# Mixture-of-experts stage: experts in order of their token counts, three short ones with tokens listed twice, blocks of up to 1024 columns, four split slots

## The chip, the cores and the metric

The kernel runs on one core of a Trainium2 chip. The metric is the device time of one execution in microseconds, as the median of several runs; less is better. The core has TensorE (matmuls into PSUM banks of 512 float32 columns), VectorE, ScalarE, GpSimd and the sync engine SyncE, whose queue starts most of the loads.

## The reference

Two transformer blocks of two layers each over 256 tokens of width 1024. All stages but the last are the same in both kernels. The last stage is a mixture of experts: eight experts, each token goes to its best two.

```python
def swiglu(h, w_gate, w_up, w_down):
    a = jnp.einsum('bsd,df->bsf', h, w_gate)
    u = jnp.einsum('bsd,df->bsf', h, w_up)
    return jnp.einsum('bsf,fd->bsd', jax.nn.silu(a) * u, w_down)

def moe_swiglu(h, w_router, w_gate, w_up, w_down):
    ...
    for e in range(N_EXPERTS):
        out = out + combine[..., e:e + 1].astype(h.dtype) * swiglu(h, w_gate[e], w_up[e], w_down[e])
```

Gate and up are 1024 x 2816, down is 2816 x 1024, all float32: 34.6 MB an expert. `combine` is zero but for the two experts of a token.

## The kernel before

**Products in three matmuls.** Float32 operands are split into a high part (rounded to the format that the matmul takes) and a low part (what is left): ScalarE writes `w_hi` (L1892), VectorE `w_lo` (L977). `product` (L2351 to L2353) then issues high by high, high by low and low by high. The tokens' rows are split in the same way (`hT_hi`, `hT_lo`), and so are the hidden values (`hid_hi`, `hid_lo`).

**Weights in tiles.** SyncE loads weight tiles of 128 x 2048 into six raw slots of `slab`, each when VectorE's low part of the tile that was there is done. A tile is then split into one of three split slots of `w_hi` and `w_lo`, each when TensorE has used the tile that was there (`w_used`). There are 33 tiles an expert.

**An expert.** Its tokens are at most 128: VectorE makes a 0/1 matrix from their places (`lists`), TensorE makes the list of token numbers from it (`list_places`), GpSimd fetches the rows by an indirect transfer (`fetch`), TensorE turns them (`turn_fetched`, L2841). The 2816 hidden columns go in six steps of at most 512: `rows_up(j)` makes the step's up rows in one bank and its gate rows in another, ScalarE takes the silu (L2279), VectorE multiplies (L1757), `turn(j)` transposes the product in pieces of 128 columns (L2470), ScalarE and VectorE split it (L2179, L1559), and `sums` adds its share of the down product in banks 2 and 3. Between a step's rows and its turn stand the sums of the step before. ScalarE scales the finished sums into `y_out` (L2263), and GpSimd adds them to `y_rows` in HBM by an indirect transfer that adds (`scatter`, L924). The last expert's sums go back by matmuls instead. Experts run in the order of their numbers; `each_expert` writes out the first and the last and loops over pairs between them. The order of the work on every engine is written out by hand. If an expert has more than 128 tokens, `flag` makes the whole stage run a second time.

Of the kernel before, what the change touches and what calls it, by code (L numbers as in the profile page):

```python
# [9 lines left out]
F32 = mybir.dt.float32  # L10
# [7 lines left out]
P = 128  # L18
D = 1024
# [47 lines left out]
F_WIDE = 512  # L67
# [22 lines left out]
X_MACT, X_MACT2, X_G, X_YE = 4096, 4864, 4608, 5376  # L90
# [114 lines left out]
def build(nc, A, out):  # L205
    ctx = ExitStack()
    with ctx:
# [10 lines left out]
        hT_lo = sb("hT_lo", [P, KC, SEQ], F32R)  # L218
        big = sb("big", [P, ADA])
# [13 lines left out]
        posi = sb("posi", [P, TT], I32)  # L233
# [7 lines left out]
        flag = sb("flag", [1, 1], I32)  # L241
# [77 lines left out]
        last_g, rows_out, rows_in = sem("last_g"), sem("rows_out"), sem("rows_in")  # L319
# [29 lines left out]
        MT = 3 * MJ  # L349
        MS = 1 + (FF2 - F_GATED) // F_WIDE  # L350
# [4 lines left out]
        def ff_tiles(l):  # L355
            return 4 * steps(l) if l < DEPTH else MT
# [165 lines left out]
        def expert_ring(ring, i, p, t0, loads0, ahead=2):  # L522


            done = MT * p + ahead
            ring.t, ring.i, ring.raw, ring.split = t0 + i * (2 * MT) + done, done, MORE_RAW, 3
            ring.at = 0 if isinstance(i, int) and i == 0 and p == 0 and t0 == ring.start else -MORE_RAW
            ring.loads = [c + i * (2 * MT // MORE_RAW) + sum(k % MORE_RAW == s for k in range(done))
                          for s, c in enumerate(loads0)]
# [10 lines left out]
        def expert_steps(eng, ring, step, before_last):  # L540

            with eng.Fori(0, MS - 3) as jj:
                ring.enter(jj, 6)
                step(jj + 2)
            ring.leave(MS - 3)
            before_last()
            step(MS - 1)

        def narrow(j):

            return isinstance(j, int) and j == 0

        def wide_at(j):

            return j * F_WIDE - F_GATED

        def expert_after(t0, loads0):

            return t0 + NE * MT, [c + NE * MT // MORE_RAW for c in loads0]
# [19 lines left out]
        def listed(p, b):  # L579

            return slice(KC // 2 * p + 2 * b, KC // 2 * p + 2 * b + 2)
# [5 lines left out]
        def by_two(src):  # L587

            return src.rearrange("p (a n) -> p a n", a=2)
# [4 lines left out]
        def _(sp):  # L594
# [82 lines left out]
            for l in LAYERS:  # L677
# [57 lines left out]
                else:  # L735
                    stage(MORE_RAW)

                    def expert_loads(t0, loads0, n0):
# [5 lines left out]
                        def body(i, p, n, first, last):  # L744
# [3 lines left out]
                            def step(j, norm=False):  # L748
                                cols(wu, wide_at(j + 1), F_WIDE)
                                if norm:  # L750

                                    sp.wait_ge(sc_done, 2 * (UNIT0[l] + UNITS[l]))
# [2212 lines left out]
```

## Time and profile before

| | |
|---|---|
| median of 3 runs | 1911.68 us (1910.37 to 1918.38) |
| profiled execution, span | 1912.1 us |
| TensorE matmul, busy | 1824.1 us, 95% |
| VectorE | 1416.6 us, 74% |
| ScalarE | 1122.6 us, 59% |
| GpSimd | 392.8 us, 21% |
| HBM read | 497.49 MB |
| the chain that ended last, by engine | PE 83%, DVE 7%, issue 6%, ACT 3%, POOL 1% |

The span runs from the first to the last instruction of one profiled execution; no other time of that execution is given. Shares of busy time are means over stages with different limits, so the stage that the change touches has to be read by itself: the experts, from about 1134 us to the end.

### The profile page before, as it was taken

Reading aid. Unit: us, or ns where it says so; the run is one execution under the profiler, and the core shown is the slowest. Engines: PE = TensorE matmul, PEld = TensorE weight load, DVE = VectorE, ACT = ScalarE, POOL = GpSimd, SP = SyncE. Lnnn points to the kernel's source line nnn. Section 1 sums busy time; section 2 is a strip of 40 time slices with the busy share of each in tenths; the row PEclk is TensorE's granted clock in tenths of the full one; section 3 lists DMA queues with packets and bytes.
Section 4 is the critical chain, followed back from the end, with each engine's and each line's share of the span. In section 5 each row is a group of like instructions: output and inputs, shape, how many; then the busy total and the mean of one; then the engine's idle time right before and its main releaser. Section 6 shows DMA issues by size and latency. Waiting matters only on the chain.

```text
span 1912.1 us, 26024 instructions
## 1 busy us (share of the span) xinstructions
PE 1824.1 (95%) x8799; PEld 1486.2 (78%) x8799; DVE 1416.6 (74%) x1631; ACT 1122.6 (59%) x1296; POOL 392.8 (21%) x315
## 2 busy tenths in 40 slices
PE   7899999989999998899989879999999999999997
PEld 6678886868888786688878667888888888888885
DVE  5748874466976586644458758889888888888897
ACT  6745444564443464443345537777777777777775
POOL 3722203463212363200046500000000000000000
PEclk9999999999999999999999989999999999999999
DMA  8348884418987341455544258999999999999994
GB/s 271 111 161 327 343 342 147 149 54 323 344 347 275 91 152 45 154 195 179 192 154 142 69 187 334 386 376 386 380 384 376 383 383 381 380 374 381 381 387 167
DMA packets 237934, 506.45 MB, mean 265 GB/s; under 512 B 23304, under 2 KB 74720, under 8 KB 231712
## 3 DMA queue, kind: packets, MB, share of 16 engines
q1 hardware_dynamic: 225664, 492.91, 70.9%
q0 software_dynamic: 3008, 10.32, 2.0%
q10 hardware_dynamic: 9184, 2.23, 0.5%
q8 instruction: 43, 0.70, 0.1%
q14 instruction: 35, 0.29, 0.0%
HBM read 497.49 MB, written 7.91 MB: 264 GB/s over the span
## 4 chain that ended last, share of the span: by engine, by line
PE 83%; DVE 7%; issue 6%; ACT 3%; POOL 1%; DMA 0%; POOLq 0%; SPq 0%; DVEq 0%; ACTq 0%
PE bank L2351 25%; PE bank L2353 25%; PE bank L2352 25%; PE bank L2470 2%; ACT slab L2042 1%; PE bank L2789 1%; DVE slab L1290 1%; PE bank L2561 1%; PE bank L2539 1%; ACT w_hi L1892 1%; PE bank L2521 1%; POOL w_lo L826 1%; DVE x L1074 0%; PE bank L2572 0%; DVE slab L1271 0%
## 5 line engine op out<-in xcount | busy, mean ns | idle before, releaser
L977 DVE TENSOR_TENSOR w_lo<-slab,w_hi 128x2048 fp32r<-128x2048 f32 x369 | 847.8, 2308 | 214.3 <-ACT w_hi L1892 213.3
L1892 ACT ACTIVATE w_hi<-slab 128x2048 fp32r<-128x2048 f32 (+2 forms) x421 | 796.6, 1898 | 329.0 <-PE bank L2353 256.3
L2351 PE MATMUL bank<-w_hi,hT_hi 128*128 128x512 f32 (+3 forms) x1664 | 649.4, 390 | 14.2 <-DVE hT_lo L1012 4.4
L2352 PE MATMUL bank<-w_lo,hT_hi 128*128 128x512 f32 (+3 forms) x1664 | 638.0, 383 | 0.0
L2353 PE MATMUL bank<-w_hi,hT_lo 128*128 128x512 f32 (+3 forms) x1664 | 637.9, 383 | 0.0
L2351 PEld LDWEIGHTS bank<-w_hi,hT_hi 128*128 128x128 f32 x1664 | 316.0, 190 | 77.9 <-DVE w_lo L977 8.8
L2353 PEld LDWEIGHTS bank<-w_hi,hT_lo 128*128 128x128 f32 x1664 | 315.5, 190 | 59.7
L2352 PEld LDWEIGHTS bank<-w_lo,hT_hi 128*128 128x128 f32 x1664 | 316.3, 190 | 55.3
L826 POOL TENSOR_TENSOR w_lo<-slab,w_hi 128x512 fp32r<-128x512 f32 (+2 forms) x208 | 262.4, 1295 | 381.3 <-ACT w_hi L1892 361.6
L2351 PE MATMUL bank<-w_hi,hid_hi 128*128 128x512 f32 x680 | 265.6, 391 | 0.7 <-DVE w_lo L977 0.7
L2353 PE MATMUL bank<-w_hi,hid_lo 128*128 128x512 f32 x680 | 265.0, 390 | 0.0
L2352 PE MATMUL bank<-w_lo,hid_hi 128*128 128x512 f32 x680 | 264.5, 389 | 0.0
L2351 PEld LDWEIGHTS bank<-w_hi,hid_hi 128*128 128x128 f32 x680 | 127.6, 188 | 29.2 <-issue 2.3
L2353 PEld LDWEIGHTS bank<-w_hi,hid_lo 128*128 128x128 f32 x680 | 127.6, 188 | 26.7
L2352 PEld LDWEIGHTS bank<-w_lo,hid_hi 128*128 128x128 f32 x680 | 127.7, 188 | 26.3
L924 POOL DMA_INDIRECT y_rows<-slab,posi x7 | 16.6, 2367 | 515.6 <-ACT slab L2263 515.6
L901 POOL TENSOR_TENSOR slab<-slab 128x512 f32<-128x512 f32 x32 | 60.0, 1893 | 251.6 <-ACT slab L2188 251.6
L1577 DVE SCALAR_TENSOR_TENSOR big<-slab,csilu,big 128x2048 f32<-128x2048 f32 x42 | 103.5, 2473 | 0.0
L2042 ACT ACTIVATE slab<-slab,att 128x256 f32<-128x256 f32 x144 | 71.4, 499 | 52.3 <-DVE att L1271 43.0
L2179 ACT ACTIVATE hid_hi<-bank 128x512 fp32r<-128x512 f32 (+1 forms) x95 | 47.6, 527 | 46.1 <-PE bank L2470 46.1
L1290 DVE TENSOR_TENSOR slab<-slab,att 128x512 f32<-128x512 f32 x56 | 52.7, 942 | 5.8
L1271 DVE CUSTOM_DVE_ANT_0 slab<-bank,const 128x256 f32<-128x256 f32 x88 | 31.9, 417 | 33.4 <-PE bank L2521 33.3
(252 smaller groups left out, 1232.0 us busy)
## 6 DMA issues: line engine op xcount, KB each, us to landing
slab<-in_w_exp_gate SPq DMA_DIRECT2D x176, 512.0 KB, 7.0
slab<-in_w_exp_up SPq DMA_DIRECT2D x176, 512.0 KB, 7.5
slab<-in_w_exp_down SPq DMA_DIRECT2D x176, 512.0 KB, 7.1
slab<-in_w_ada SPq DMA_DIRECT2D x48, 1024.0 KB, 5.5
slab<-in_w_mlp_in SPq DMA_DIRECT2D x64, 512.0 KB, 5.4
slab<-in_w_mlp_out SPq DMA_DIRECT2D x64, 512.0 KB, 9.0
slab<-in_w_in SPq DMA_DIRECT2D x56, 512.0 KB, 5.0
slab<-in_w_out SPq DMA_DIRECT2D x32, 512.0 KB, 4.6
```

What stands on the lines that cost most here:

```text
L826: ins = pool.tensor_tensor(w_lo[:, q, o], raw(s)[:, o], w_hi[:, q, o].bitcast(F32), ALU.subtract)
L901: pool.tensor_tensor(scr(X_ACT2 + t * F_UP, F_UP), a, a, ALU.mult).then_inc(sq_done, 1)
L977: dve.tensor_tensor(w_lo[:, q, 0:n], raw(s)[:, 0:n], w_hi[:, q, 0:n].bitcast(F32), ALU.subtract).then_inc(lo_dve, 1)
L1290: dve.tensor_tensor(p, p, r[:, s, :].unsqueeze(2).broadcast_to([P, TT, SEQ]), ALU.mult).then_inc(nrm_done, 2)
L1577: ins = dve.scalar_tensor_tensor(acc, w, c, acc, ALU.mult, ALU.add)
L1892: act.activation(w_hi[:, q, 0:n], raw(s)[:, 0:n], ACT.Copy).then_inc(hi_done, 1)
L2042: act.activation(p, p, ACT.Exp, bias=att[:, 1, j, t:t + 1], scale=-1.0, accum_out=att[:, 2, j, t:t + 1]).then_inc(ex_done, 1)
L2179: act.activation(to_hi[:, f0:f0 + n, t * P:(t + 1) * P], src, ACT.Copy).then_inc(hidh_done, 1)
L2351: pe.matmul(dst, a_hi, b_hi, start=start, stop=False)
L2352: pe.matmul(dst, a_hi, b_lo, start=False, stop=False)
L2353: return pe.matmul(dst, a_lo, b_hi, start=False, stop=stop_)
L2470: ins = pe.transpose(dst[t][:, f * P:(f + 1) * P], scr(src + t * width_ + f * P, P), ident)
```

## The change

- The experts are sorted by their numbers of tokens in a new piece of code on VectorE (`sort`). Expert 0 is always first. Of the others the four with the most tokens take the odd places 1, 3, 5 and 7, and the three with the fewest the places 2, 4 and 6. These three are the short ones. SyncE reads the order from `order` and picks the weights by it.
- A short expert has at most 64 tokens, and its list names each of them twice, in columns 0 to 63 and 64 to 127. Its gate is made in full, with three matmuls a product, for both copies. Its up product takes as rows 64 high parts and 64 low parts of the same tokens, so two matmuls (by `w_hi` and by `w_lo`) do for three. Both halves are multiplied by the gate, and the turn adds them: instead of a transpose, each chunk of 128 columns takes two matmuls by halves of the identity matrix. The hidden values are then stacked in the same way for the down product, and the two halves of its result are added to `y_rows` by two indirect transfers. The down product of the last block, which is issued in the next expert's body, stays at three matmuls, with `hid_lo` cleared.
- All experts work in three blocks of 768, 1024 and 1024 hidden columns, in two banks for gate (0, 1) and two for up (4, 5), up first. A row of a load of gate or up is 4 KB (3 KB in the first block), where it was 2 KB (1 KB in the first step). There are 36 tiles an expert, 12 of them narrower than 2048 columns or half full.
- Four split slots instead of three.
- SyncE's loads are written out expert by expert instead of looped over.

```diff
+E_WIDTH = (768, 1024, 1024)
+MS = len(E_WIDTH)
+MT = 36
+SHORT = P // 2
+SHORT_AT = (2, 4, 6)
...
-                    ring.stage(3 if l < MOE else MORE_RAW, 3, 1)
+                    ring.stage(*((3, 3, 1) if l < MOE else (MORE_RAW, SPLIT, 0)))
...
+            def down_chunks(j):
+
+                return ((0, 2), (2, 2), (4, 1), (5, 1)) if j == 0 else ((0, 2), (2, 2), (4, 2), (6, 2))
...
+                                for k in range(2):
+                                    sp.dma_start(d[:, k:k + 1, :], w[:, 2 * b + k:2 * b + k + 1, E_FROM[j]:E_FROM[j] + E_WIDTH[j]]
+                                                 ).then_inc(loaded, 16)
...
+                for a, o in enumerate((slice(0, SHORT), slice(SHORT, P)) if at in SHORT_AT else (slice(0, P),)):
+                    pool.wait_ge(scattered, done - (16 if at not in SHORT_AT else 32) + 16 * a)
...
+                        hidden_low(0)
+                        if short:
+                            dve.wait_ge(w_used, FREE_SPLIT + EXPERT0 + n * MT + 8)
+                            dve.tensor_scalar(hid_lo[:, :, :], ones[:, 0:1].unsqueeze(2).broadcast_to([P, 4, SEQ]), 0.0, None, ALU.mult
+                                              ).then_inc(hid_zero, 1)
+                        if first:
+                            dve.nop().then_inc(hid_zero, 1)
+                        if first and n0 == 0:
+                            sort()
...
+                        def both(dst, hi_, lo_, q, s, start, stop_):
+
+                            if lo_ is None:
+                                pe.matmul(dst, hi_, w_hi[:, q, s], start=start, stop=False)
+                                return pe.matmul(dst, hi_, w_lo[:, q, s], start=False, stop=stop_)
+                            return product(dst, hi_, lo_, w_hi[:, q, s], w_lo[:, q, s], start, stop_)
...
+                                    if halved:
+                                        l_hi, l_lo = rows_k[:, SHORT:SHORT + P], None
+                                    else:
+                                        l_hi, l_lo = rows_k[:, 0:P], rows_k[:, P:2 * P]
...
+                                if short:
+                                    to = banks[f // 4][:, f % 4 * P:f % 4 * P + SHORT]
+                                    pe.matmul(to, src, ident[:, 0:SHORT], start=True, stop=False)
+                                    ins = pe.matmul(to, src, ident[:, SHORT:P], start=False, stop=True)
+                                else:
+                                    ins = pe.transpose(banks[f // 4][:, f % 4 * P:(f % 4 + 1) * P], src, ident)
...
+                        inner(0)
+                        gate(0)
+                        if first:
+                            inner(1)
+                            pe.wait_ge(ix_made, 2 * n + 2)
+                            turn(0)
+                        else:
+                            if p == 1:
+                                pe.wait_ge(hid_zero, i + (1 + (len(SHORT_AT) + 1) * turn_))
+                            sums(-1, False)
+                            turn(0)
+                            inner(1)
+                        gate(1)
```

Where instructions move, the order on the engine shows it. First TensorE, before, from the end of one step's sums over its turn into the next step's up rows (every expert, inside the loop; L2470 is the turn, L2351 to L2353 a product):

```order
L2351 MATMUL bank<-w_hi,hid_hi 128x512
L2352 MATMUL bank<-w_lo,hid_hi 128x512
L2353 MATMUL bank<-w_hi,hid_lo 128x512
L2468 REGISTER_ALU
L2470 MATMUL bank<-const,slab 128x128 x4
L2884 REGISTER_ALU
L2404 ISA
L2351 MATMUL bank<-w_hi,hT_hi 128x512
```

And the same place in a short expert of the change, with the numbers of the banks (L3113 and L3114 are the two halves of the turn, L3054 and L3055 the two matmuls of an up product; the sums ahead of this turn are those of the expert before, in three matmuls, L2533 to L2535):

```order
L2535 MATMUL bank3<-w_hi,hid_lo 128x512
L3109 ISA
L3113 MATMUL bank0<-const,big 128x64
L3114 MATMUL bank0<-const,big 128x64
...
L3048 REGISTER_ALU
L3054 MATMUL bank4<-w_hi,hT_hi 128x512
L3055 MATMUL bank4<-w_lo,hT_hi 128x512
L3054 MATMUL bank5<-w_hi,hT_hi 128x512
L3055 MATMUL bank5<-w_lo,hT_hi 128x512
```

The turn of four transposes has become one of six (in the other blocks eight) pairs of narrow matmuls, and the products after it have lost their third matmul.

Second VectorE, before, in the first expert (L977 is a low part of a weight tile, L1757 the multiplication, L1559 the low part of the hidden values, L1706 and L1700 the list of the next expert):

```order
L1741 TENSOR_TENSOR hT_lo<-bank,hT_hi 128x512 x2
L1730 TENSOR_SCALAR listed_cols<-bank,listed_cols 128x1
L1731 COPY listed_cols<-bank 128x1
L1733 SCALAR_TENSOR_TENSOR posi<-bank,listed_cols 128x1
L977 TENSOR_TENSOR w_lo<-slab,w_hi 128x2048
L1757 TENSOR_TENSOR slab<-slab,bank 128x256
L977 TENSOR_TENSOR w_lo<-slab,w_hi 128x2048 x2
L1559 TENSOR_TENSOR hid_lo<-bank,hid_hi 128x2x128
L977 TENSOR_TENSOR w_lo<-slab,w_hi 128x2048 x2
L1706 COPY listed_cols<-big 128x2
L1700 TENSOR_SCALAR slab<-const,big 128x128 x2
L977 TENSOR_TENSOR w_lo<-slab,w_hi 128x2048
```

And in the change (L1847 is the low part of a tile, L1857 the multiplication, L1874 the hidden low part; L1771 to L1795 are the sort, 25 instructions, of which the first and the last stand here):

```order
L1847 TENSOR_TENSOR w_lo<-slab,w_hi 128x1536 x6
L1847 TENSOR_TENSOR w_lo<-slab,w_hi 128x2048 x3
L1857 TENSOR_TENSOR big<-slab,bank 128x384 x2
L1847 TENSOR_TENSOR w_lo<-slab,w_hi 128x2048 x4
L1874 TENSOR_TENSOR hid_lo<-bank,hid_hi 128x512
L1874 TENSOR_TENSOR hid_lo<-bank,hid_hi 128x256
L1771 COPY big<-const 128x1
...
L1795 CAST posi<-big 1x1
L1803 COPY listed_cols<-big 128x2
L1805 TENSOR_SCALAR slab<-const,big 128x128 x2
L1847 TENSOR_TENSOR w_lo<-slab,w_hi 128x2048 x3
L1847 TENSOR_TENSOR w_lo<-slab,w_hi 128x1024
```

Nine low parts now stand ahead of the first multiplication, and the sort stands between the first hidden low part and the list of the second expert, with tile 15's low part behind it.

## Rows read from the trace of the kernel before

**Rows 1.** The page: busy time, tenths in 40 slices, transfer rates

```profile
PE 1824.1 (95%) x8799; PEld 1486.2 (78%) x8799; DVE 1416.6 (74%) x1631; ACT 1122.6 (59%) x1296; POOL 392.8 (21%) x315
...
PE   7899999989999998899989879999999999999997
...
GB/s 271 111 161 327 343 342 147 149 54 323 344 347 275 91 152 45 154 195 179 192 154 142 69 187 334 386 376 386 380 384 376 383 383 381 380 374 381 381 387 167
```

**Rows 2.** Chain that ended last, 1200 to 1420 us: start, length, what

```profile
1217.05 0.87 PE bank L2841 x8
...
1310.34 0.44 PE bank L2470 x4
1310.78 0.87 PE bank L2841 x8
...
1404.51 0.87 PE bank L2841 x8
```

**Rows 3.** Busy time by stretch; columns as its first row names them

```profile
core 0: us, PE busy (x) PEld busy (x) DVE busy (x) ACT busy (x) POOL busy (x), PEclk, DMA share, GB/s
1140.00:1150.00 10.00, 8.31 (x33) 6.46 (x32) 3.90 (x6) 4.17 (x4) 0.00 (x0) 0.83 0.62 216
...
530.00:540.00 10.00, 10.00 (x46) 8.29 (x45) 7.35 (x4) 4.99 (x4) 3.01 (x2) 1.00 1.05 413
1359.00:1387.00 28.00, 28.00 (x127) 23.20 (x126) 25.20 (x17) 20.66 (x13) 0.98 (x1) 1.00 1.05 396
1335.00:1429.00 94.00, 94.00 (x433) 77.99 (x432) 84.07 (x54) 70.90 (x50) 3.35 (x2) 1.00 1.04 382
```

**Rows 4.** Waits, 1335 to 1429 us: total, times, longest

```profile
ACT w_hi L1892 <- PE bank L2353: 13.3, 21, 1.2
DVE w_lo L977 <- ACT w_hi L1892: 9.7, 21, 0.9
...
PEld bank L2470 <- DVE slab L1757: 0.2, 1, 0.2
```

**Rows 5.** Waits of the load queue in the same stretch

```profile
SPq L626 <- DVE w_lo L977: 52.6, 33, 2.8
```

**Rows 6.** Groups by form, 1335 to 1429 us: busy, mean ns | idle

```profile
L977 DVE TENSOR_TENSOR w_lo<-slab,w_hi 128x2048 fp32r<-128x2048 f32 x34 | 77.5, 2292 | 9.8 <-ACT w_hi L1892 9.7
L1892 ACT ACTIVATE w_hi<-slab 128x2048 fp32r<-128x2048 f32 x34 | 65.2, 1917 | 13.3 <-PE bank L2353 13.3
...
L1559 DVE TENSOR_TENSOR hid_lo<-bank,hid_hi 128x512 fp32r<-128x512 f32 x5 | 3.4, 683 | 0.0
```

**Rows 7.** TensorE in order of time, expert stage: start, length (six starts)

```profile
1343.55 0.39 PE L2351 MATMUL bank<-w_hi,hT_hi 128*128 128x512 f32 x1
...
1344.91 0.39 PE L2351 MATMUL bank<-w_hi,hT_hi 128*128 128x512 f32 x1
```

**Rows 8.** TensorE in order of time, an attention stage: other widths

```profile
1054.16 0.33 PE L2353 MATMUL bank<-w_hi,hT_lo 128*128 128x384 f32 x1
...
1055.20 0.33 PE L2353 MATMUL bank<-w_hi,hT_lo 128*128 128x384 f32 x1
...
1057.98 1.00 PE L2549 MATMUL bank<-big,slab 128*128 128x64 f32 x8
1058.79 0.42 PE L2351 MATMUL bank<-w_hi,hT_hi 128*128 128x384 f32 x1
```

**Rows 9.** Transfers: an MLP stretch (530 to 540), then 1335 to 1429

```profile
DMA packets 1213, 4.13 MB, mean 413 GB/s; under 512 B 103, under 2 KB 103, under 8 KB 1082
...
DMA packets 16562, 35.94 MB, mean 382 GB/s; under 512 B 1097, under 2 KB 3145, under 8 KB 16558
```

**Rows 10.** VectorE in order of time, routing: linked small instructions

```profile
1129.32 0.29 DVE L1679 TENSOR_TENSOR slab<-slab 128x128 f32<-128x128 f32 x1
1129.65 0.29 DVE L1680 TENSOR_REDUCE big<-slab 128x16 f32<-128x128 f32 x1
```

**Rows 11.** TensorE in order of time, first expert's start, with idle before

```profile
1150.90 0.44 PE L2470 MATMUL bank<-const,slab 128*128 128x128 f32 x2 [0.93 <-DVE slab L1757]
...
1154.57 0.50 PE L2351 MATMUL bank<-w_hi,hT_hi 128*128 128x512 f32 x1 [0.48 <-DVE w_lo L977]
```

**Rows 12.** Issues of GpSimd, 1250 to 1850 us: median us to landing

```profile
big<-y_rows POOLq DMA_DIRECT2D x1, 1024.0 KB, 9.2
y_rows<-slab,posi POOLq DMA_INDIRECT x7, 10.5
```

More of the change, by code:

```diff
@@ L520, in build @@
         g_tables = rowg[:, 0:8 * HD].rearrange("p (a t d) -> p a t d", a=4, t=TT)
[L522 to L529, printed above, removed]
+        mact, mact2 = scr(X_MACT, max(E_WIDTH)), big[:, B_MACT2:B_MACT2 + max(E_WIDTH)]
+        EXPERT0 = FF0[MOE]
+        EXPERT_LO = FREE_RAW + EXPERT0 - len(POOLED)
         def each_expert(eng, n0, body):
@@ new lines, in expert_loads @@
+                        before = None
+                        for n in range(n0, n0 + NE):
+                            first, last = n == n0, n == n0 + NE - 1
+                            if n == n0 + 1:
+                                sp.wait_ge(order_done, 1)
+                            wg, wu, wd = weights(0 if first else sp.value_load(order[0:1, n - n0:n - n0 + 1], min_val=0, max_val=NE - 1))
+                            wide_rows(wu, 0, n, up_tile(0, first))
+                            if n == 0:
+                                sp.wait_ge(sc_done, 2 * (UNIT0[l] + UNITS[l]))
+                            wide_rows(wg, 0, n, gate_tile(0, first))
+                            if not first:
+                                down_rows(before, -1, n)
+                            wide_rows(wu, 1, n, up_tile(1, first))
+                            wide_rows(wg, 1, n, gate_tile(1, first))
+                            down_rows(wd, 0, n)
+                            if n == 0:
@@ L1694, in _ @@
                 link(dve.tensor_scalar(pos, pos, -1.0, None, ALU.add))
-                def matches(e, signal):
-                    pe_ = pos[:, :, bass.ds(e, 1)]
-                    for t in range(TT):
-                        dve.tensor_scalar(scr(X_G + t * P, P), iota, pe_[:, t], None, ALU.is_equal).then_inc(signal, 1)
-                def lists(e, n):
+                ranked_wts, ranked_pos = rt[:, 10], rt[:, 11]
+                counts, turns = rt[:, 12, 0, :], rt[:, 13, 0, :]
+                rank_at, spare = rt[:, 12, 1, :], rt[:, 13, 1, :]
@@ L1768, in body, with lows @@
-                        step(0, ahead=int(first))
-                        if last:
-                            last_lists(n)
-                        else:
-                            lists(2 * i + p + 1, n + 1)
-                        step(1, ahead=1)
-                        if not last:
-                            make_index(1 - p, n + 1, not first)
+                        short = is_short(p, first)
+                        def lows(r0, r1):
+                            for r in range(r0, r1):
+                                w, s, q = tile_width(r, first, last), raw_slot(r), split_slot(r)
+                                dve.wait_ge(hi_done, n * MT + (EXPERT0 + r + 1))
+                                dve.tensor_tensor(w_lo[:, q, 0:w], raw(s)[:, 0:w], w_hi[:, q, 0:w].bitcast(F32), ALU.subtract
+                                                  ).then_inc(lo_dve, 1)
```

560 lines of the change are left out of this document (339 added, 221 removed).

## Prediction

> **What bounds the kernel now.** I read the page first. The last third of the span is the expert stage: from slice 25 TensorE is busy 9 tenths or more, and the transfers too, near 380 GB/s, while before that both go up and down [rows 1]. So two things could set its pace, and the next views have to tell which. The chain that ended last is, in this stage, an unbroken row of matmuls: the eight turns of the fetched rows (L2841), one each expert, stand 93.73 us apart (1217.05, 1310.78, 1404.51) [rows 2]. In one expert's stretch TensorE is busy 94.00 of 94 us at clock 1.00, VectorE 84.07, ScalarE 70.90, and 382 GB/s are moved [rows 3]. The waits of that stretch say who is ahead of whom: TensorE waits 0.2 us in all, ScalarE waits 13.3 us for TensorE to free a split slot, VectorE 9.7 us for ScalarE [rows 4], and the queue of loads waits 52.6 us for VectorE to free a raw slot [rows 5]. Nobody waits for a transfer. The period also comes out of the matmuls: six starts in 1.36 us are 0.2267 us each [rows 7], 396 of them are 89.8 us, 22 turns at 0.11 (0.44 for four) are 2.4 and the turn of the fetched rows 0.87 [rows 2]. TensorE is the bound, with VectorE 10% behind it and the transfers close too. That closeness decides what the change is worth.
>
> **Taken out: matmuls of three experts.** A short expert (places 2, 4 and 6) does its up product and the down product of its first two blocks with two matmuls where there were three. The third block's down product is issued in the next expert's body, with three, and `hid_lo` is cleared for it. Per short expert 76 matmuls go, 60 of 512 columns at 0.2267 us and 16 of 384 columns. Six starts of that width took 1.04 us, so 0.173 each [rows 8]. That is 13.6 + 2.8 = 16.4 us.
>
> **Added in the turn.** Each of its 22 chunks is no longer one transpose but two plain float32 matmuls of 64 columns. The trace has this form: eight records, four matmuls, between 1057.98 and 1058.79, so 0.20 us each [rows 8] and 0.405 a pair, against 0.11 before. This gives back 22 x 0.295 = 6.5 us. The bounds are 0.11 a chunk (nothing added) and 0.45. The other widths (384 and 512 for 256 and 512) make 420 matmuls out of 396 in every full expert: 324 x 0.2267 + 96 x 0.1733 = 90.1 for 89.8, +0.3 us. TensorE's work in a short expert is 93.7 - 16.4 + 6.5 + 0.3 = 84.1 us.
>
> **The other engines in a short expert.** VectorE's low parts cost 2.292 us at 2048 columns, and its hidden low part 0.683 at 512 [rows 6], so 1.05 ns a column and 0.15 a start. It gets three more starts (36 tiles for 33, +0.4), half the hidden columns (1408 fewer, -1.5) and the clearing of 1024 columns (some +1.0): 83.8 us a period in rows 3 becomes 83.7. ScalarE stays near 70. The loads: an expert moves 35.94 MB in 94 us in 16562 packets, 2170 bytes each. A 10 us stretch of the MLP stage with 3405 bytes a packet (1213 packets, 4.13 MB) [rows 9] moved 413 GB/s at share 1.05, while 28 us of the expert stage away from most of the indirect traffic moved 396 at the same share [rows 3]. After the change gate and up rows are 4 or 3 KB, for 2 and 1 KB before, and I count 9216 rows of 3750 bytes for the weights of an expert where there were 15104 of 2290. So 35.84 MB take 86.8 us at 413, 90.5 at 396, and 93.8 at 382, which is the present pace. I take 413, the row whose packets are nearest. The three limits of a short expert are then 84.1, 83.7 and 86.8, and I take 86.8 as its length. It saves 6.9 us, not the 16.4 of its matmuls, and three save 20.8 us. The full experts stay with TensorE: five times +0.3 is +1.5. At 86.8 against 94.0 us the loads regain there what they lost.
>
> **Does the even flow hold?** Low parts are made ahead of TensorE by what the slots allow. With three slots a tile is begun two tile times (2 x 2.72) before its use and needs 1.92 + 2.29: 1.2 us spare. With four it is 3.95 us spare. In a short expert four up tiles pass at 8 x 0.2267 = 1.81 us against VectorE's 2.29, which draws 1.9 us of it. Gate tiles, at 2.72, give it back. So I put no stall there in the forecast, and 1 to 2 us a short expert if the block's multiplications (2 x 0.68) and listed rows fall on the same place. The blocks are twice as wide, so silu, multiplication and turn come 3 times an expert, not 6, each behind the sums of the block before. These last 5.4 us at the least (sums of block 0 in a short expert: two tiles at 1.81, two at 0.91). The chain that they hide is at most a low part under way (2.29), and two multiplications (0.68 each): 3.7 us.
>
> **The sort.** 25 small instructions of VectorE stand between the first hidden low part and tile 15 of the first expert. Linked ones of this kind start 0.33 us apart at 128 columns [rows 10], and shorter at 8 to 64: I take 5.7 us together. They are hidden by the tiles that are ready: when the first turn ends TensorE has tiles 12 to 14, 8.2 us. VectorE needs 2.1 (hidden high and low) + 5.7 + 0.7 (lists) + 2.3 (low part of tile 15) = 10.8. What is late is tile 15, by **2.5 us** (bounds 0, if the sort runs at 0.15 an instruction, and 5). Behind it everything shifts, since TensorE is the bound there.
>
> **The start and the end.** At the start TensorE waited 0.93 us for the first multiplication and 0.48 for a low part [rows 11]. The new order puts `inner(1)` between gate and turn, and a fourth slot: -1.4. The slow clock there (0.83 in the first 10 us, [rows 3]) stays. The sums of the last short expert (place 6) now need two indirect adds, one after the other, 10.5 us each, before they are read back, 9.2 [rows 12]. In the last expert TensorE is done with them at 27.4 us (16 up and gate products of each half at 384 columns, 16.6, then 16 products of 0.68), the copy ends at 28.7, and the sums are there at 59. VectorE wants them after the low part of tile 24, which follows tile 20's use at 61.8 by 1.92 + 2.29: 66. No cost; it takes 7 us more to be one. Clearing in three transfers and the loads of the expert numbers are on queues that wait anyway.
>
> **Sum.** -20.8 + 1.5 + 2.5 - 1.4 = -18.2 us. The profiled execution's span is 1912.1, 0.4 above the median of the three timed runs (1911.7), and no other time of it is given. So 1911.7 - 18.2 = **1893.5 us**. Likeliest case's own range 1887 to 1901.
>
> **Rivals.**
> (a) Loads and VectorE hide fully behind 84.1 us, because a short expert lives on what was loaded ahead (the loads land and wait now, rows 5). Then 3 x 9.6 = 28.8 saved, no stall at the sort: 1911.7 - 28.8 + 1.5 - 1.4 = 1883. For it: six raw slots. Against it: 36 smaller tiles share them. Chance 0.12.
> (b) The transfers cap: the larger rows bring only the 396 of the expert stage itself. 90.5 us, 3.2 saved each: 1911.7 - 9.7 + 1.5 + 2.5 - 1.4 = 1904.6. For it: share 1.04 to 1.05 all through. Against it: 52.6 us in which the queue only waited for slots. Chance 0.15.
> (c) No more than the present 382: nothing saved, 1914. Chance 0.06. The Trainium skill, HBM Reference, "Specifications (TRN2)", gives about 358 GB/s as a core's share of its HBM. By that rule the weights alone would need an estimated 97 us an expert, and relieving TensorE would be worth nothing. This trace does not agree (382 over a whole expert, 413 at best). The same section's figure for a core that streams alone, about 425, fits it better.
> (d) Slower: the wide blocks. Where a block's multiplications queue behind two low parts, the turn comes late, and TensorE stops at each of 24 block ends. At the two waits of rows 11 together, 1.4 us each, that is +34: 1927. It decides from 0.76 us a block end, which eats the 18.2. Against it: the cover of 5.4 us and more, worked out above. Chance 0.08.
> (e) The change does not do what it says: an expert in a short place with over 64 tokens makes `flag` start a second round, some 740 us more. By the reference's routing of these inputs the experts have 23, 54, 101, 78, 97, 44, 51 and 64 tokens; expert 0 goes first, and 54, 51 and 44 are the short ones. Chance under 0.01; other mishaps 0.02.
> The forecast has 0.56.
>
> **Range and chances.** 0.5% is 9.6 us, about what a measurement of this kernel can tell from no change, so faster begins under 1902.1. Faster: 0.54 of the forecast, 0.12, and a little of (b): 0.71. Within: most of (b), part of (c), 0.18. Slower: (d) and mishaps, 0.11. The range runs from (a), 1883, to past (b), 1908, and leaves out (c), (d), (e) and the far ends.
>
> **What would show it.** In the profile after: the turns of fetched rows 94 us apart after full experts and 87 after short ones; in short ones TensorE idle some 3% and waiting for `w_lo`, behind it ScalarE waiting for a load at last; rates of 400 GB/s and more over a pair of experts. The turn's pairs at 0.4 us. One TensorE wait of 2 to 3 us near 1180, in expert 0. I am wrong if short experts last 84 (a), 90 or more with ScalarE waiting for loads (b, c), or if TensorE's waits stand ahead of the turns (d).

## The result: 0.9% slower, where 1.0% faster was forecast

| | median | runs | against before (95% interval) |
|---|---|---|---|
| before | 1911.39 us | 4, 1910.37 to 1918.38 | |
| after | 1928.81 us | 4, 1925.48 to 1937.85 | 1.0087 [1.0056, 1.0119] |
| forecast | 1893.5 us | range 1883 to 1908 | |

The time is 35 us above the forecast and outside its range. The profiled execution has a span of 1926.6 us, 14.5 more than that of before.

### The profile after

From the page, the lines that answer to [rows 1], and of its DMA queues the one that carries instructions (packets, MB, share):

```profile
PE   7899999989999998899989879999989998999997
...
DMA  8348884428897331555554239999989998999994
GB/s 269 110 167 328 341 342 137 149 72 310 345 346 268 94 132 45 175 182 188 169 169 138 99 127 372 374 399 367 399 326 392 357 399 339 391 359 399 380 400 169
...
q8 instruction: 66, 1.08, 0.2%
```

From slice 29 on, slices that lie inside an expert, short or full, show 391 to 400 GB/s, and those across the border between two experts 326 to 380. In two of the latter (slices 30 and 34) TensorE is no longer at 9 tenths. The instruction queue had 43 packets before. It looks like nothing, and turned out to be the largest single cause.

The rows that answer to [rows 3] are the windows of a short expert (place 2) and of the full one behind it, and, from other questions of the same kind, the 72 us in which the loads run hardest and the first 5.66 us of the full expert:

```profile
core 0: us, PE busy (x) PEld busy (x) DVE busy (x) ACT busy (x) POOL busy (x), PEclk, DMA share, GB/s
1328.72:1421.60 92.88, 89.03 (x447) 75.23 (x445) 82.76 (x57) 69.41 (x52) 5.12 (x2) 0.98 1.01 387
1426.34:1522.84 96.50, 96.50 (x455) 83.50 (x455) 80.72 (x53) 68.59 (x49) 6.51 (x3) 0.97 0.94 353
...
1342.00:1414.00 72.00, 68.71 (x334) 56.42 (x332) 65.62 (x47) 56.19 (x43) 5.12 (x2) 1.00 1.03 401
...
1426.34:1432.00 5.66, 5.66 (x18) 5.66 (x19) 0.00 (x0) 1.42 (x1) 0.00 (x0) 0.53 0.55 193
```

The short expert lasts 92.9 us, not 86.8. Then TensorE stands until 1426.34, and the full expert lasts 96.5 instead of the 94.0 forecast; its first multiplications run at a mean granted clock of 0.53, near the 1.2 GHz level. What TensorE does there, in order of time (start, length, idle before):

```profile
1411.52 0.39 PE L3055 MATMUL bank<-w_lo,hid_hi 128*128 128x512 f32 x1
1414.39 0.60 PE L3054 MATMUL bank<-w_hi,hid_hi 128*128 128x512 f32 x1 [2.48 <-DVE w_lo L1847]
1414.79 0.63 PE L3055 MATMUL bank<-w_lo,hid_hi 128*128 128x512 f32 x1
1415.21 0.63 PE L3054 MATMUL bank<-w_hi,hid_hi 128*128 128x512 f32 x1
...
1426.34 0.68 PE L2533 MATMUL bank<-w_hi,hT_lo 128*128 128x384 f32 x1 [4.74 <-DVE w_lo L1847]
1426.82 0.52 PE L2534 MATMUL bank<-w_lo,hT_lo 128*128 128x384 f32 x1
1427.14 0.52 PE L2535 MATMUL bank<-w_hi,hT_lo 128*128 128x384 f32 x1
```

There are two stalls. One of 2.48 us stands ahead of tile 31, the last of a short expert's down tiles in block 1; behind it the matmuls start 0.43 us apart, where [rows 7] have 0.2267. It is there in all three short experts (1414.39, 1608.19, 1800.33). VectorE in the same place, in order of time:

```profile
1407.45 2.29 DVE L1847 TENSOR_TENSOR w_lo<-slab,w_hi 128x2048 fp32r<-128x2048 f32 x1 [0.27 <-ACT w_hi L2419]
1409.66 1.28 DVE L1857 TENSOR_TENSOR big<-slab,bank 128x512 f32<-128x512 f32 x2
1410.86 1.28 DVE L1833 TENSOR_TENSOR hT_lo<-bank,hT_lo 128x512 fp32r<-128x512 f32 x2
1412.05 7.29 DVE L1847 TENSOR_TENSOR w_lo<-slab,w_hi 128x2048 fp32r<-128x2048 f32 x4
```

Between the low parts of tiles 30 and 31 stand the block's two multiplications (L1857) and two listed rows (L1833). Tile 31's low part starts at 1412.05 and takes 2.29 us, so it is there at 1414.34. The other stall, 4.74 us, stands at the end of TensorE's loop body. It comes again at 1619.40 with 3.98 us, but not at 1807.33, between the same kinds of expert. There the loop is left and not repeated. The releaser printed for it is VectorE's low part of tile 35, but `inner(0)` begins with tile 32, whose low part had long been made. When the engine that is printed had long been done, the wait was for something else.

Ahead of the expert stage two more rows differ from before. First ScalarE, then VectorE, at the norm:

```profile
1116.03 2.85 ACT L2030 ACTIVATE w_hi<-slab 128x1536 fp32r<-128x1536 f32 x2 [16.22 <-PE bank L2535]
1118.80 0.61 ACT L2061 ACTIVATE h<-x 128x512 f32<-128x512 f32 x1
```

```profile
1113.99 0.69 DVE L1131 TENSOR_TENSOR x<-slab,x 128x512 f32<-128x512 f32 x1
1119.53 0.15 DVE L1140 TENSOR_SCALAR stat<-stat 128x1 f32<-128x1 f32 x1 [4.85 <-ACT h L2061]
```

ScalarE makes the high halves of the first two expert tiles ahead of the norm's squares. With four split slots counted from slot 0, they need the slots of the last output tiles. So the squares, ready from 1112, stand behind a wait of 16.22 us, and VectorE waits 4.85 us for them. Before, the two halves were made at 1096.6 and 1103.4, in the time in which ScalarE had to wait anyway.

The theories that came out of this are for three places: the jump back of TensorE's loop (theory 1, the code), the order of the splits at the end of a short expert (theory 2 puts the 4.74 us down to it, theory 3 the 2.48), and the squares. Theories 4 and 5 say what is left in a short expert: TensorE's work with its waits, or its bytes.

### The profile page after: what moved, and what is told of

Same layout as the page of the kernel before. It is cut to its first block, busy times and chain, and to the rows that moved or that the text cites. A ratio compares the mean times of both kernels' runs of the same rounds, so it can differ in the third digit from the quotient of the medians.

```text
span 1926.6 us, 25985 instructions
## 1 busy us (share of the span) xinstructions
PE 1817.2 (94%) x8961; PEld 1502.3 (78%) x8961; DVE 1415.8 (73%) x1679; ACT 1119.5 (58%) x1320; POOL 404.7 (21%) x320
## 4 chain that ended last, share of the span: by engine, by line
PE 67%; DVE 11%; DMA 8%; issue 7%; ACT 5%; POOL 1%; SPq 0%; DVEq 0%; POOLq 0%; ACTq 0%
PE bank L2533 20%; PE bank L2535 19%; PE bank L2534 19%; DMA slab<-in_w_exp_down 4%; DVE w_lo L1847 3%; DMA slab<-in_w_exp_up 3%; ACT w_hi L2419 2%; ACT slab L2180 1%; PE bank L2967 1%; DVE slab L1347 1%; PE bank L2739 1%; PE bank L2648 1%; PE bank L2717 1%; PE bank L2699 1%; ACT w_hi L2030 1%
## 5 line engine op out<-in xcount | busy, mean ns | idle before, releaser
L1847 DVE TENSOR_TENSOR w_lo<-slab,w_hi 128x2048 fp32r<-128x2048 f32 (+2 forms) x286 | 594.3, 2114 | 68.5 <-ACT w_hi L2419 66.7
L2535 PE MATMUL bank<-w_hi,hT_lo 128*128 128x512 f32 (+3 forms) x1336 | 503.7, 377 | 0.0
L2533 PE MATMUL bank<-w_hi,hT_hi 128*128 128x512 f32 (+3 forms) x1208 | 463.4, 384 | 15.1 <-DVE hT_lo L1083 4.2
L2534 PE MATMUL bank<-w_lo,hT_hi 128*128 128x512 f32 (+3 forms) x1208 | 455.7, 377 | 0.0
L1034 DVE TENSOR_TENSOR w_lo<-slab,w_hi 128x2048 fp32r<-128x2048 f32 x105 | 245.7, 2350 | 136.7 <-ACT w_hi L2030 136.7
L2535 PEld LDWEIGHTS bank<-w_hi,hT_lo 128*128 128x128 f32 x1336 | 254.7, 191 | 41.1
L2533 PEld LDWEIGHTS bank<-w_hi,hT_hi 128*128 128x128 f32 x1208 | 230.2, 191 | 59.7 <-issue 7.2
L2534 PEld LDWEIGHTS bank<-w_lo,hT_hi 128*128 128x128 f32 x1208 | 230.6, 191 | 35.5
L2533 PE MATMUL bank<-w_hi,hid_hi 128*128 128x512 f32 x588 | 230.1, 391 | 0.0
L2535 PE MATMUL bank<-w_hi,hid_lo 128*128 128x512 f32 x588 | 229.2, 390 | 0.0
L2533 PE MATMUL bank<-w_hi,hT_lo 128*128 128x512 f32 (+1 forms) x384 | 145.5, 379 | 8.7 <-DVE w_lo L1847 8.7
L2534 PE MATMUL bank<-w_lo,hT_lo 128*128 128x512 f32 (+1 forms) x384 | 144.0, 375 | 0.0
L2533 PEld LDWEIGHTS bank<-w_hi,hid_hi 128*128 128x128 f32 x588 | 110.4, 188 | 24.2 <-issue 2.0
L2535 PEld LDWEIGHTS bank<-w_hi,hid_lo 128*128 128x128 f32 x588 | 110.4, 188 | 23.2
```

The lines of the kernel that those rows point to most:

```text
L1034: dve.tensor_tensor(w_lo[:, q, 0:n], raw(s)[:, 0:n], w_hi[:, q, 0:n].bitcast(F32), ALU.subtract).then_inc(lo_dve, 1)
L1847: dve.tensor_tensor(w_lo[:, q, 0:w], raw(s)[:, 0:w], w_hi[:, q, 0:w].bitcast(F32), ALU.subtract).then_inc(lo_dve, 1)
L2533: pe.matmul(dst, a_hi, b_hi, start=start, stop=False)
L2534: pe.matmul(dst, a_hi, b_lo, start=False, stop=False)
L2535: return pe.matmul(dst, a_lo, b_hi, start=False, stop=stop_)
```

## The experiments

### The jump back: TensorE's loop written out in the kernel before, and left out in the kernel after

In `b_unroll`, the kernel before, TensorE's inner loop alone is changed. Its other engines keep theirs.

```
-                        with pe.Fori(0, MS - 3) as j:
-                            ring.enter(j, 6)
+                        ring.enter(0, 6)
+                        for j in range(MS - 3):
                             rows_up(j + 2)
```

> The kernel before, with TensorE's loop over three of an expert's six blocks written out: the same multiplications and waits in the same order, but the loop over experts grows on TensorE from 552 to 856 matrix multiplications, as many as in the kernel after (850). Theory 1 (code): the kernel after stood for 4.74 and 3.98 us at its two jumps back because its loop body is no longer kept in the engine and is fetched anew. Then this kernel fetches instructions all through 1400 to 1750 us, where before fetched none, stands 4 to 5 us at each of two jumps, and takes 10 to 14 us more than before: 1922 to 1925. Theory 2 (order of the splits): the 4.74 us are a wait for the low half of the up tile that is split behind the hidden rows of the last block. Then nothing changes here: 1911 within 3.

It took 1923.72 us, 1.0071 [1.0045, 1.0097] of before, or 12.0 us more for the same work. TensorE in order of time at the first jump:

```profile
1422.93 0.49 PE L2470 MATMUL bank<-const,slab 128*128 128x128 f32 x3
1426.94 0.50 PE L2351 MATMUL bank<-w_hi,hT_hi 128*128 128x512 f32 x1 [3.52 <-issue]
1427.28 0.39 PE L2352 MATMUL bank<-w_lo,hT_hi 128*128 128x512 f32 x1
```

The profile now says it itself: no semaphore, "issue". The second jump cost 2.98 us. The DMA view of 1400 to 1750 us has this row, and that of before has no such row at all:

```profile
q8 instruction: 17, 0.28, 0.3%
```

So only the queue q8 moved (its packets in the whole execution went from 43 to 66, those of the other instruction queue stayed at 35), and only TensorE's code was changed. From one turn of the fetched rows to the next, the two stretches that hold a jump lasted 99.1 and 98.6 us, and all others 93.7 as before. That is 10.2 us of the 12.0: 6.5 of standing, and 3.7 behind it, where the granted clock was at its lower level. The stalls are shorter than the 4 to 5 us expected. The theory of split order can explain none of it. The code theory stands.

The branch itself has a record in the view of the loop's line. Before (L535), in `b_unroll` (L535) and in the kernel after (L540), shortest, median and longest in ns:

```profile
L535 PEldq COMPARE_BRANCH  x3: 76/207/208, 1419.8 to 1794.7; - x3
...
L535 PEldq COMPARE_BRANCH  x3: 83/5082/5610, 1421.0 to 1806.2; - x3
...
L540 PEldq COMPARE_BRANCH  x3: 83/5762/6512, 1419.5 to 1805.5; - x3
```

A jump back took 0.2 us before, and 5.1 to 6.5 us in the two others. The shortest of the three is the last, which isn't taken. TensorE stands for less than the branch takes, since 2.1 to 2.4 us of matmuls are still ahead of it when the branch begins.

In `no_jump`, the kernel after, TensorE's loop over experts is written out:

```
-                    each_expert(pe, n0, body)
+                    for i in range(NE):
+                        body(i // 2, i % 2, n0 + i, i == 0, i == NE - 1)
```

> The kernel after, with TensorE's loop over the experts written out, so that TensorE has no jump in the expert layer. Theory 1 (code): the 4.74 and 3.98 us at the jumps back go, and with them the half clock behind each (16 multiplications at 0.32 instead of 0.17 us, some 2.4 us each): 1928.8 less 11 to 14, 1915 to 1918. Theory 2 (order of the splits): it stays at 1928.8 within 3, with the stall of 4.7 us still ahead of the first up tile of experts 3 and 5.

It took 1915.41 us, 13.4 under the kernel after. Both stalls at the jumps are gone, and the full experts behind them last 94.0 us again, for 96.5 and 95.6:

```profile
1331.98:1425.19 93.21, 88.92 (x447) 0.98 1.01 385
1425.19:1519.20 94.01, 94.01 (x457) 1.00 0.99 379
```

(Windows of TensorE alone: us, busy, clock, DMA share, GB/s.) Instructions are fetched here almost as often, 14 packets from 1400 to 1750 us for 16. Here fetching cost nothing that shows while the code went straight on; only the jump did. From experts' lengths in the two traces some 12 us of the 13.4 come back at the two jumps: 4.4 and 3.3 us in the short experts that hold them, 2.5 and 1.6 in the full ones behind.

In `b_unroll_one` the inner loop is written out in one of the loop body's two experts only:

```
+                        if p:
+                            ring.enter(0, 6)
+                            for j in range(MS - 3):
+                                step(j)
+                        else:
                             with pe.Fori(0, MS - 3) as j:
```

> The kernel before with TensorE's loop over three blocks written out in one of the two experts of the loop body only: 704 multiplications in the body, between the 552 of before (no instructions fetched from 1400 to 1750 us, no stall at the jumps) and the 856 with both written out (fetched all through, 3.5 and 3.0 us at the jumps). Theory 1 with a bound of size: either it behaves like the one (1911, nothing fetched) or like the other (about 1918 to 1924, fetched all through); nothing between is expected, since a body that doesn't stay is fetched from its start. The row on instruction packets tells which. I take the first as a little likelier.

It took 1910.52 us, ratio 1.0 [0.9985, 1.0014]. From 1400 to 1750 us it fetched one packet (`q8 instruction: 1, 0.02, 0.0%`), and no wait at the jumps is in its list. So a loop body of 704 multiplications stays in the engine, and those of 850 and 856 don't. Its jumps back took 0.2 us, as before.

`fewer_bytes_loop` asks what the stall is made of. It is `fewer_bytes`, told of further down, which loads only half of the gate weights and so computes other products, with the loop of the kernel after:

```
-                    for i in range(NE):
-                        body(i // 2, i % 2, n0 + i, i == 0, i == NE - 1)
+                    each_expert(pe, n0, body)
```

> fewer_bytes with TensorE's loop over experts kept as a loop, as in the kernel after. The jump back is made while the loads run at 351 GB/s on average instead of 390. Theory 1a (the stall is the time to fetch at the jump, whatever else moves): 3 to 4 us stand at each of the two jumps, and the half clock follows: 9 to 13 us over fewer_bytes. Theory 1b (the fetch is slow because it queues behind saturated loads): under 1 us at each jump, within 4 us of fewer_bytes.

It took 1897.02 us, 6.8 over `fewer_bytes`, between the two expectations. (Four and five runs of different rounds don't tell 6.8 from 4; the experts' lengths in the two traces give 6.4.) The stalls are 2.44 and 2.07 us. So neither version of the theory is the whole. The traces hold ten slow jumps, in five kernels, and each can be taken apart into the time from the branch's start to the start of its instruction packet, the packet, and the rest of the branch:

| | to the packet | packet | rest |
|---|---|---|---|
| `fewer_bytes_loop`, 2 jumps | 1.5 | 0.9 to 1.2 | 1.5 |
| the kernel after, `b_unroll`, `squares_first`, `list_later`, 8 jumps | 2.6 to 4.1 | 0.9 to 1.1 | 1.5 |

Only the wait ahead of the packet differs. It is shortest where the loads moved some 240 GB/s in that time, and longer where they moved 295 to 386. That this wait is queueing behind the loads fits, but among the eight it doesn't follow the rate, and no run shows it by itself.

The Trainium skill, Runtime: NRT & Kernel Launch, "Instruction fetch mechanics", has the rule. Instructions come in blocks of 16 KiB, straight on they are fetched ahead, and a taken jump out of what is held waits for a fetch. The trace agrees (16 packets in 350 us, and a stall at each of two jumps). The section gives PE room for 2048 instructions and in another sentence speaks of two blocks only. By the first, an estimate of two instructions a multiplication and some hundred others puts the body of 704 at 1500, that of 856 in `b_unroll` at 1800, and that of 850, with its doubled float32 ones, near 1900. All three would fit, and the last two weren't held. By the second none would stay, and the run with 704 speaks against it. Neither sentence draws the line where the runs have it, between some 1500 and 1800 instructions by the estimate.

### The squares first

`squares_first`, the kernel after with ScalarE's order turned:

```
-                    hi(2 * E_WIDTH[0] if l == MOE else TILE)
-                    if l == MOE:
-                        hi(2 * E_WIDTH[0])
+                    if l < MOE:
+                        hi()
...
                     square_halves()
...
+                    else:
+                        hi(2 * E_WIDTH[0])
+                        hi(2 * E_WIDTH[0])
                     turn()
```

> The kernel after, with the high halves of the first two up tiles of the expert layer made behind the squares of the norm on ScalarE, and not ahead of them. Theory: the two halves waited 16.2 us for the split slots of the last output tiles (four slots from slot 0 now), the squares stood behind them, and VectorE waited 4.85 us for the first square. With the order turned, the wait ahead of VectorE's L1140 row goes, and the time falls by 4 to 5 us: 1924 to 1925. Rival: the layer's first expert waits for its first up tile instead, since its halves now come behind the norm, or its loads; then no gain, 1928.8 within 2.

It took 1920.99 us, 7.8 less by the medians. ScalarE and VectorE in order of time:

```profile
1111.90 0.63 ACT L2061 ACTIVATE h<-x 128x512 f32<-128x512 f32 x1 [13.73 <-DVE x L1131]
...
1117.90 2.85 ACT L2030 ACTIVATE w_hi<-slab 128x1536 fp32r<-128x1536 f32 x2
```

```profile
1114.44 0.21 DVE L1140 TENSOR_SCALAR stat<-stat 128x1 f32<-128x1 f32 x2
```

VectorE's wait is gone, and no wait for the first up tile came in its place. The gather of the first expert starts at 1135.71 for 1139.96. That alone is little proof, since this start moves by several us between executions. The time from the block's first residual addition (1110.61 in the kernel after) to the gather doesn't: it is 29.2 to 29.4 us in the three traces with the old order, and 24.3 to 25.3 in the seven with the new. So 4 to 5 us are shown, as expected. The 7.8 of the medians are more than expected, and the rest of it has no place in the traces.

### The order at the end of a short expert

`list_later`, the kernel after with tile 31 ahead of the listed rows, on ScalarE (`highs`) and in the same way on VectorE (`lows`):

```
-                                listed_rows(1 - p, n + 1)
-                                highs(31, 35)
+                                highs(31, 32)
+                                listed_rows(1 - p, n + 1)
+                                highs(32, 35)
```

> The kernel after, with the first down tile of the second block (tile 31) split ahead of the next expert's listed rows on ScalarE and VectorE, and not behind them. Theory 3 (order at the end of a short expert): the 2.48 us stall at the last of the four down tiles of block 1 goes in the three short experts, and with it most of the half clock that follows it (14 multiplications at 0.43 and some at twice 0.2, about 3 us): 4 to 5 us for each, 1914 to 1917. Rival (transfers): the loads run at 401 to 413 GB/s over the whole short expert and tile 31 would only be late by its bytes; the wait then moves to the next tiles and the time stays at 1926 to 1930.

It took 1918.79 us, 10.0 less. The 2.48 us have become 1.28, and from one expert's first up tile to the next it was 94.21 (with the jump), 94.31 and 90.13 us for 97.62, 96.56 and 92.33: 7.9 us over the three. The theory hit the place. The gain is short of the 12 to 15 expected, for two reasons: tile 31 is still late by what ScalarE's silu (1.07 us) and VectorE's multiplication (1.28) take, and 2.0 of the 7.9 us are shorter stalls at the two jumps (3.56 and 3.21), which this edit doesn't aim at.

### The three together

`all_three` has the three edits in one kernel.

> The three edits of the last runs together in the kernel after: TensorE's loop over the experts written out, the squares ahead of the first up tiles' high halves, tile 31 split ahead of the listed rows. They act at different places (13.4, 7.8 and 10.0 us by the medians), so theory: they add up, 1928.8 less 25 to 31, 1898 to 1904, 8 to 14 us under the kernel before. Full experts at TensorE's 94.0 us, short ones at 90 to 90.7. Rival: what one frees another takes (the transfers run at their limit and take back what TensorE no longer waits for), 1908 to 1914.

It took 1899.93 us, 0.994 [0.9917, 0.9962] of before: 28.9 under the kernel after, and 11.3 us faster than before. The three nearly add up; singly they gave 13.4 + 7.8 + 10.0 = 31.2. The windows of a short and a full expert:

```profile
1319.77:1409.34 89.57, 87.07 (x447) 73.98 (x446) 81.88 (x57) 69.55 (x52) 4.87 (x2) 1.00 1.01 391
1409.34:1503.35 94.01, 94.01 (x456) 81.01 (x456) 83.78 (x57) 70.67 (x52) 6.52 (x3) 1.00 1.01 387
```

The full expert is as forecast, the short one 2.8 us above its 86.8.

### What sets a short expert: order, work or bytes

`ahead` goes on from there: tile 31 also ahead of silu and multiplication.

```
-                            highs(23, 31)
+                            highs(23, 32)
                             activated(2)
```

> all_three, and tile 31 split ahead of the block's activation too (so too tile 19 in the block before), on ScalarE and VectorE. In the run with tile 31 ahead of the listed rows alone, TensorE still stood 1.28 us for it, since ScalarE made the activation first (1.07 us) and VectorE the product (1.28 us). Theory (order): the 1.28 us go, and with them what the clock loses behind them in the short experts, 1.3 to 3 us for each: 4 to 9 us under all_three. Rival (transfers): the loads at 401 to 413 GB/s make the tile late by themselves, and the wait moves: within 2 us of all_three.

It took 1903.25 us (1898.27 to 1906.09), no gain over `all_three`, whose six runs reach from 1897.85 to 1903.97. The 1.28 us are gone from TensorE's waits, short experts last 89.2, 89.1 and 89.7 us, and ScalarE waits for loads 16.1 us in one where it waited 13.3. The wait had only moved, as the rival has it.

`half_turn` takes work away from TensorE instead. The half sums of the three short experts are left out.

```
-                                    pe.matmul(to, src, ident[:, 0:SHORT], start=True, stop=False)
-                                    ins = pe.matmul(to, src, ident[:, SHORT:P], start=False, stop=True)
+                                    ins = pe.matmul(to, src, ident[:, 0:SHORT], start=True, stop=True)
```

> all_three without the second of the two multiplications that turn a chunk of 128 hidden columns in a short expert, so that the half sums are not made (the result of three experts is left out of the sum). It takes 22 times 0.2 to 0.22 us, 4.4 to 4.9 us, of TensorE's work from each of three experts. Theory 4 (TensorE and its waits set a short expert): 12 to 15 us under all_three. Theory 5 (a short expert is set by its bytes): 35.9 MB at the 409 GB/s that the loads reached there are 88 us against 90 to 90.7 measured, so no more than 6 to 8 us under all_three, and TensorE's waits for low halves grow by the rest.

It took 1899.0 us, 0.9 under `all_three`, with some 14 us of multiplications fewer. Short experts: 89.3, 88.8 and 88.7 us. ScalarE's waits in the first of them (us in total, times, longest):

```profile
ACT w_hi L2422 <- DMA slab<-in_w_exp_gate: 7.4, 7, 1.9
ACT w_hi L2422 <- DMA slab<-in_w_exp_down: 5.3, 7, 1.3
ACT w_hi L2422 <- DMA slab<-in_w_exp_up: 4.7, 6, 1.6
```

17.4 us of waiting for loads, for 13.3 in `all_three`. What TensorE no longer has to do, a short expert doesn't gain: it stays at 88.7 to 89.3 us.

`fewer_bytes` takes bytes away instead: of every second row block of the gate weights only 64 columns are loaded, in all experts.

```
+                                    n_ = 64 if part and k else E_WIDTH[j]
```

> all_three with only 64 columns loaded of every second row block of the gate weights (the rest of the tile keeps what another tile left there, so its product is not that of the reference), in all experts: 16 per cent fewer bytes for an expert. Theory 5 (bytes): TensorE's short waits of 0.3 to 1.3 us for low halves go, 2.8 us in each short expert, and the half clock behind the last of them, 3 to 4 us for each of three: 9 to 12 us under all_three; full experts stay at 94.0. Theory 4 (TensorE): the waits are due to the order in which ScalarE and VectorE make the splits and stay: within 3 us of all_three.

It took 1890.2 us, 9.7 under `all_three`. The window of its first short expert:

```profile
1323.52:1409.39 85.87, 85.61 (x448) 74.44 (x446) 82.17 (x57) 68.82 (x52) 5.10 (x2) 1.00 0.96 351
```

TensorE is busy throughout, so 85.9 us is its own work in a short expert. Theory 5 hit in both directions: a short expert is set by its bytes.

One thing is left open. In a short expert of `all_three` the queue of loads still waits for VectorE to free a raw slot (us in total, times, longest):

```profile
SPq L789 <- DVE w_lo L1847: 33.0, 23, 2.5
SPq L800 <- DVE w_lo L1847: 19.2, 10, 4.1
SPq L803 <- DVE w_lo L1847: 2.4, 2, 1.2
```

So ScalarE waits for loads, and loads are issued only as slots come free, with a DMA share of 1.01 where the MLP stretch of [rows 3] has 1.05. Whether the 391 GB/s are what the transfers can do, or what six raw slots let them do, no run tells. A kernel with another number of raw slots would.

`full_products` gives TensorE the whole work in short experts (`short = False` in its body; hidden rows are still split in halves, so three experts' results are not the reference's).

> all_three with TensorE's full work in the three short experts: three multiplications each in up and down and plain transposes instead of the stacked halves (ScalarE and VectorE still split the hidden rows in halves, so the result of the three is not that of the reference). Theory 5 (bytes): in all_three a short expert was set by its bytes at 89.6 to 89.9 us, so the halves gained only 94.0 less 89.7, 4.3 us each, and this kernel takes 13 us more, 1911 to 1915, with 94.0 us for every expert and no stall. Rival: the transfers would run dry in full experts also, now that nothing lets them catch up, and it is over 1917.

It took 1914.4 us, ratio 1.0005 [0.9991, 1.0019] of before, with every expert at 93.98 to 94.01 us. So all that the stacked halves bring is the difference to `all_three`: 13 us by the experts' lengths, and 12 to 14.5 by the times (`before` had 1911.23 in the round of one and 1913.42 in that of the other). Without them the new tiling, with all three repairs, is worth nothing.

## Why the prediction was wrong

**What it left out: the code.** The largest piece is in no step: the prediction put TensorE's jump back at nothing, without a word. The working counted what TensorE's matmuls take, and not how many of them stand in the text of its loop. The change writes out what was a loop over three blocks, and the body grows from 552 multiplications to 850. Two jumps, 8.7 us, and the clock behind them, some 4 us (full experts of 96.5 and 95.6 for 94.0): 13.4 us in the run without the loop. The order of TensorE's instructions showed it: an inner branch that was there before, and isn't after.

**"The start": -1.4 us** missed what lies ahead of it. The two waits of [rows 11] did go. But the step looked at TensorE in the first expert only, and the fourth split slot put a wait on ScalarE ahead of the norm: +4 to 5 us by the rows, 7.8 by the medians. What it should have asked is whose slot the first `hi` takes, and what stands behind it on its engine.

**"Does the even flow hold?"** named the place: "1 to 2 us a short expert if the block's multiplications and listed rows fall on the same place", and put it at nothing in the forecast. They do fall there. It was 2.48 us, and the clock fell to its lower level behind it; 10.0 us came back when half of it was undone, some 2 of them at the jumps. The slack of 3.95 us was worked out for an engine that is never late, but ScalarE was already waiting for loads (0.64 us each ahead of two down tiles at 1402.94 and 1405.50), so the down tiles came 2.56 us apart. And the step let only the up tiles draw on the slack and the gate tiles give it back. The down tiles, which follow, draw on it too: TensorE needs some 1.9 us for one (eight starts from 1409.80 to 1411.52).

**The bytes: 86.8 us.** The mechanism was right, in that bytes set a short expert, and the size wrong: 88.7 to 89.3 us (`half_turn`), and 89.7 with TensorE's waits. The 413 GB/s came from a 10 us stretch. The changed kernel reaches 401 to 413 in all but one of the twelve windows of 6 us between 1342 and 1414, but 401 over 72 us and 387 to 391 over an expert, in which the indirect transfers and a start with full slots lie. This is 2.9 us in each of three, 8.7 us, more than the 6.4 that separate `all_three` (1899.9) from the forecast; the sort's smaller stall (-0.9) goes against it. That kernel is at the place between forecast and rival (b).

**What held.** Full experts 94.0 us, +0.3 as put. TensorE's own work in a short expert 85.9 for 84.1; a turn's pair took 0.446 us for 0.405, at the upper bound given, which is half of these 1.8 us. The sort stalled TensorE once, at 1188.00, by 1.57 us for 2.5. The last sums made nobody wait. Rival (d), the wide blocks, cost nothing ahead of any turn. Rival (c) is out: 391 GB/s over an expert, in which the loads set the pace. The share of about 358 GB/s that the Trainium skill, HBM Reference, "Specifications (TRN2)", gives doesn't bind here; the trace doesn't agree with it.

**The sum in hindsight.** From the forecast of 1893.5: jumps 13.4, squares 7.8, order 10.0, bytes 8.7, sort -0.9 make 1932.5. The three edits together gave 2.3 us less than singly, which makes 1930.2, for 1928.8 measured. The first three terms are measured differences between kernels and fit by construction. What this sum tests is the rest, 7.8 us by the rows for 6.4 by the medians.

## What to carry to other kernels

Where a change replaces a loop by written-out code, or the reverse, count the instructions of the body that is jumped back over, engine by engine, and look for instruction packets in the DMA queues: none in a steady loop means that it is held, and a steady stream with an "issue" wait at the jump means that it isn't. Then write the outer loop out as well, or keep the body small. And where slots are added, ask of each engine what now stands behind its first use of the new slot. When an engine is relieved next to transfers that are near their limit, take the rate from a stretch as long as the one forecast, and expect small order stalls to be the first to show, since the slack that hid them is gone.

## What the runs showed of the hardware

A loop body of TensorE with 704 multiplications was fetched once and then held (1 packet of instructions in 350 us, 0.2 us a jump back); with 850 or 856, 16 and 17 packets came in 350 us, and TensorE stood 3.0 to 4.7 us at each jump back, 2.1 and 2.4 with fewer bytes loaded. The branch itself took 3.8 to 6.5 us: 1.5 to 4.1 until its packet started, about 1 for the packet, and 1.5 more. The same code without the jump, fetched almost as often (14 packets), cost nothing that shows. Behind a stall of 4.74 us that followed one of 2.48, TensorE ran 5.66 us at a mean granted clock of 0.53, and its expert took 2.5 us more; in `all_three`, with waits of 1.3 us at most in that stretch, the clock stayed at 1.00.
